# The last output projection of a two-block transformer: twelve of its sixteen column tiles in pairs, by seven products of halves

## What is computed

```python
def odd_layer(x, norm_g, w_in, q_gain, k_gain, sinks, w_out, rel_bias):
    h = rms_norm_2(x, norm_g) @ w_in
    q, k, v, gate = split_cols_2(h, ODD_SPLITS)
    ...
    o = swa_sink_attention(q, k, v, sinks, rel_bias)
    return x + (jax.nn.silu(gate) * o) @ w_out        # [512,2048] @ [2048,2048]
```

## Time and profile before

| | us |
|---|---|
| median of 3 runs (lowest, highest) | 2705.16 (2702.83, 2705.91) |
| the profiled execution | 2701.84 |
| its span | 2700.1 |
| PE busy | 2657.8 (98%) |
| DVE, ACT, POOL busy | 1139.1 (42%), 993.2 (37%), 1262.3 (47%) |

### The profile page before, as it was taken

The page is one execution under the profiler, slowest core; times in us unless marked ns, Lnnn a source line. Parts: engine busy times, 40 slices in busy tenths (PEclk is TensorE's granted clock), DMA queues, the critical chain, the costliest instruction groups (busy, mean ns, idle before and its releaser), DMA issues.

```text
span 2700.1 us, 34253 instructions
## 1 busy us (share of the span) xinstructions
PE 2657.8 (98%) x13651; PEld 2136.9 (79%) x13651; DVE 1139.1 (42%) x1857; ACT 993.2 (37%) x1582; POOL 1262.3 (47%) x655
## 2 busy tenths in 40 slices
PE   7999999999999999999999999999999999999999
PEld 4678988888888777888877778677888887777887
DVE  3257344146530427322123577554223445666311
ACT  4342522242242335322233123664222335666311
POOL 1236135235513537455433445776564555444443
PEclk9999999999999999999999999999999999999999
DMA  9853253225682322365332333324443333222543
GB/s 369 312 187 107 79 159 82 60 83 194 190 120 67 94 63 78 92 147 133 98 95 78 103 85 100 89 78 138 125 123 96 92 92 100 79 79 79 152 118 89
DMA packets 502237, 317.38 MB, mean 118 GB/s; under 512 B 100560, under 2 KB 456656, under 8 KB 499264
## 3 DMA queue, kind: packets, MB, share of 16 engines
q1 hardware_dynamic: 444720, 280.66, 36.2%
q10 hardware_dynamic: 57360, 34.54, 5.5%
HBM read 298.26 MB, written 29.41 MB: 121 GB/s over the span
## 4 chain that ended last, share of the span: by engine, by line
PE 94%; POOL 2%; DVE 1%; ACT 1%; issue 1%; SPq 1%; DMA 1%; DVEq 0%; ACTq 0%; POOLq 0%
PE acc L2252 81%; PE aux L2252 7%; PE ssq L2255 3%; PE ssq L2252 2%; POOL w_lo L1364 1%; DMA ada_ring<-in_w_ada 1%; DVE rstd L1719 0%; PE aux L2255 0%; SPq L773 0%; ACT p_t L1181 0%; ACT w_hi L1033 0%; POOL nbr_bias L1434 0%; POOL staged_lo L1381 0%; DVE gate_rows L1812 0%; PE acc L2255 0%
## 5 line engine op out<-in xcount | busy, mean ns | idle before, releaser
L1364 POOL TENSOR_TENSOR w_lo<-raw,w_hi 128x1024 fp32r<-128x1024 f32 x362 | 877.7, 2425 | 1221.4 <-ACT w_hi L1033 1221.3
L2252 PE MATMUL acc<-h_hi,w_hi 128*128 128x512 f32 (+1 forms) x3232 | 1188.1, 384 | 4.5 <-DVE k_t L1731 1.5
L2252 PE MATMUL acc<-h_hi,w_lo 128*128 128x512 f32 (+1 forms) x3232 | 1170.6, 379 | 0.0
L2252 PE MATMUL acc<-h_lo,w_hi 128*128 128x512 f32 (+1 forms) x2464 | 872.0, 376 | 0.0
L1033 ACT ACTIVATE w_hi<-raw 128x1024 fp32r<-128x1024 f32 x362 | 383.8, 1060 | 1057.6 <-PE acc L2252 1034.1
L2252 PEld LDWEIGHTS acc<-h_hi,w_hi 128*128 128x128 f32 x3232 | 583.9, 188 | 152.0 <-issue 34.9
L2252 PEld LDWEIGHTS acc<-h_hi,w_lo 128*128 128x128 f32 x3232 | 583.7, 188 | 117.3
L2252 PEld LDWEIGHTS acc<-h_lo,w_hi 128*128 128x128 f32 x2464 | 439.9, 188 | 82.5 <-issue 1.9
L2252 PE MATMUL acc<-out_t_lo,w_hi 128*128 128x512 f32 x768 | 298.8, 389 | 0.0
L1719 DVE RECIPROCAL rstd<-rstd 128x512 f32<-128x512 f32 (+1 forms) x29 | 118.0, 4070 | 271.3 <-ACT rstd L1085 271.2
L2252 PEld LDWEIGHTS acc<-out_t_lo,w_hi 128*128 128x128 f32 x768 | 144.2, 188 | 29.5
(11 more groups left out here) (300 smaller groups left out, 2614.5 us busy)
## 6 DMA issues: line engine op xcount, KB each, us to landing
raw<-in_w_in SPq DMA_DIRECT2D x52, 1024.0 KB, 5.9
raw<-in_even_w_in SPq DMA_DIRECT2D x41, 1024.0 KB, 5.6
raw<-in_odd_w_in SPq DMA_DIRECT2D x36, 1024.0 KB, 5.6
ada_ring<-in_w_ada SPq DMA_DIRECT2D x32, 1024.0 KB, 6.0
gate_ring<-in_w_ada SPq DMA_DIRECT2D x16, 1024.0 KB, 6.4
raw<-in_w_out SPq DMA_DIRECT2D x16, 1024.0 KB, 6.4
raw<-in_even_w_out SPq DMA_DIRECT2D x16, 1024.0 KB, 5.9
raw<-in_odd_w_out SPq DMA_DIRECT2D x16, 1024.0 KB, 5.8
```

Source lines behind the costliest of these rows:

```text
L1364: G_.tensor_tensor(WL[half][:], RAW[G.rs][:, half * HALF * P:(half + 1) * HALF * P], WH[half][:].bitcast(F32), ALU.subtract).then_inc(S["l ...
L2252: return M.matmul(out_, lhsT, rhs, start=start, stop=stop, skip_group_check=True)
```

## The change

Tiles 0 to 3 of the last stage stay as they were ("whole tiles"). Tiles 4 to 15 are done as six pairs. A pair's weights are four blocks of 1024 x 128 (a, c the upper half of the rows for the two tiles, b, d the lower half), and the gated input is four quarters (two halves of the rows, two of the tokens). A pair is then a product of 2 x 2 blocks by 2 x 2 quarters, and is done by seven products in place of eight, in the scheme of Strassen and Winograd, with s1 = c + d, s2 = s1 - a, s3 = a - c, s4 = b - s2 on the weights' side and four sums t1 to t4 on the input's. A product is 8 k-tiles x 3 matmuls of 256 columns, with its own rounded and split factor.

- The sums of the input, once: DVE makes them in two sets of eight operations (`hidden_sums`), ahead of the additions of whole tiles 1 and 2; t2, t3 and t4 are left in PSUM (`acc`, `aux`, `ssq`) and t1 in SBUF, in the place of the last four tiles of `x_t`. ACT rounds them (`sums_hi`, ahead of the stores of tiles 1 and 2), DVE makes their low parts (`hidden_lo`). t1 takes the place of the quarter it isn't needed with, so its two parts are made after the whole tiles.
- The sums of the weights, for each pair: four operations of DVE, s1 in `aux`, s2 in `ssq`, s3 and s4 in place.
- The factors: ACT rounds seven for a pair; POOL splits a, b, s3, s4 and d, DVE s2 and s1. There is a third pair of buffers for them.
- DVE adds each product's result to `x_t` (seven additions of 256 columns for a pair), then transposes the two tiles.
- SP loads blocks of 0.5 MB into a ring of six; the last load of `x_t` stands between block c and block d of pair 1 and waits until t1 is used up.

```diff
-    for j in range(KT):
+    for j in range(WHOLE):
...
+WHOLE = 4
+PAIRS = (KT - WHOLE) // 2
+PRODUCTS = ("a", "b", "s2", "s1", "s3", "s4", "d")
+BY_POOL = (0, 1, 4, 5, 6)
+BLOCK_AT = {"a": 0, "c": 1, "d": 2, "b": 3}
...
+        def wblock(s, what):
+            at_ = (4 * s + BLOCK_AT[what]) % 6
+            ring = (RAWX, RAW[third.rs], RAW[fourth.rs])[at_ // 2]
+            return ring[:, at_ % 2 * HALF * P:(at_ % 2 + 1) * HALF * P]
+        def factor(s, n):
+            return {"a": wblock(s, "a"), "b": wblock(s, "b"), "s2": SSQ[:], "s1": AUX[:], "s3": wblock(s, "c"),
+                    "s4": wblock(s, "b"), "d": wblock(s, "d")}[PRODUCTS[n]]
+        def halves(s, n):
+            slot = (7 * s + n) % 3
+            return (WHX, WLX) if slot == 2 else (WH[slot], WL[slot])
...
+        def sums_of(s, n):
+            at_ = {0: 0, 1: 768, 2: 0, 3: 512, 4: 0, 5: 512, 6: 0}[n]
+            return ACC[:, (third.c + s) % 2, at_:at_ + 256]
...
+            def pairs():
+                for s in range(PAIRS):
+                    if s == 0:
+                        sp.wait_ge(S["half_done"], gates_done)
+                    elif s == 1:
+                        sp.wait_ge(S["lo_done"], 2 * fourth.g + 2)
+                    else:
+                        sp.wait_ge(S["lo_done"], lo_pool(s - 2, 6))
+                    load(s, "a")
+                    load(s, "c")
+                    if s == 1:
+                        sp.wait_ge(S["h_full"], KT + 7)
+                        x_four(2, 3)
+                    if s == 0:
+                        sp.wait_ge(S["lo_done"], 2 * third.g + 2)
+                    else:
+                        sp.wait_ge(S["w_sums"], 4 * s - 1)
+                        sp.wait_ge(S["lo_done"], lo_pool(s - 1, 0))
+                    load(s, "d")
+                    if s:
+                        sp.wait_ge(S["lo_done"], lo_pool(s - 1, 4))
+                    load(s, "b")
...
-                        for b in range(4):
-                            sp.dma_start(tiles(X, KT, SEQ)[:, 4 * b:4 * b + 4],
-                                         xt_d[G.layer - 1][4 * b:4 * b + 4].rearrange("k p t -> p k t"))\
-                              .then_inc(S[f"xl{b}"], 16)
+                        for b in range(4 if G.kind == "wout" else 3):
+                            x_four(G.layer, b)
...
+                def sums_hi(half):
+                    act.wait_ge(S["w_fin"], 32)
+                    act.wait_ge(S["h_sum"], KT + 8 * half + 8)
+                    for t in ("t2", "t3", "t4"):
+                        (by_bank if t == "t2" else whole_bank)(lambda o, i: A.activation(o, i, ACT.Copy),
+                                                               four_k(three(SUMH[t][:]), half), SUMP[t])                            .then_inc(S["hf_hi"], 1)
+                def factor_hi(s, n):
+                    what = PRODUCTS[n]
+                    if what in "abd":
+                        act.wait_ge(block_sem(what), loaded_block(s))
+                    else:
+                        act.wait_ge(S["w_sums"], 4 * s + {"s2": 2, "s1": 2, "s3": 3, "s4": 4}[what])
+                    if 7 * s + n < 2:
+                        act.wait_ge(S["half_done"], 2 * fourth.g + n + 1)
+                    elif 7 * s + n > 2:
+                        act.wait_ge(S["half_done"], number(s, n - 3))
+                    A.activation(halves(s, n)[0][:], factor(s, n), ACT.Copy).then_inc(S["hi_done"], 1)
+                def pairs():
+                    for s in range(PAIRS):
+                        for n in range(7):
+                            factor_hi(s, n)
+                            if s == 0 and n == 2:
+                                act.wait_ge(S["half_done"], products_before)
+                                A.activation(quarter(H3H, 0, 1), three(SUM1[:]), ACT.Copy).then_inc(S["hf_hi"], 1)
+                            if s and n in (3, 4):
+                                send(WHOLE + 2 * s - 5 + n)
+                        if s == 0:
+                            send(WHOLE - 1)
+                    for j in (KT - 2, KT - 1):
+                        send(j)
...
+                    if G is third or G is fourth:
+                        sums_hi(int(G is fourth))
...
+                for s in range(PAIRS):
+                    for n in BY_POOL:
+                        high, low = halves(s, n)
+                        pool.wait_ge(S["hi_done"], number(s, n))
+                        G_.tensor_tensor(low[:], factor(s, n), high[:].bitcast(F32), ALU.subtract)\
+                          .then_inc(S["lo_done"], 1)
...
-                        need(dve, "fin_turned", j - 1)
-                        Vv.tensor_tensor(FIN[G.js][:], a, ktile(X, j, SEQ), ALU.add).then_inc(S["taken"], 1)
-                        need(dve, f"out{G.js}", 64 * (j // 2))
-                        dve.wait_ge(S["taken"], G.t + 1)
-                        Vv.transpose(FOUT[G.js][:], FIN[G.js][:]).then_inc(S["fin_turned"], 1)
+                        Vv.tensor_tensor(ktile(X, j, SEQ), a, ktile(X, j, SEQ), ALU.add).then_inc(S["taken"], 1)
+                        block_turn(j, G.t + 1)
...
+                def hidden_sums(half):
...
+                    def made_of(to, one, two, op, after_):
+                        dve.wait_ge(S["h_sum"], count + after_)
+                        split = by_bank if any(t is SUMP["t2"] for t in (to, one, two)) else whole_bank
+                        split(lambda o, a, b: Vv.tensor_tensor(o, a, b, op), to, one, two).then_inc(S["h_sum"], 1)
+                    if half == 0:
+                        dve.wait_ge(S["half_done"], gates_done)
+                        dve.wait_ge(S["ot_lo"], 2 * KT)
+                        dve.wait_ge(S["w_pt0"], 32)
+                    else:
+                        dve.wait_ge(S["h_full"], KT + 3)
+                    whole = lambda to, n, after_: made_of(to, lows[n].bitcast(F32), highs[n].bitcast(F32), ALU.add, after_)
+                    whole(rest, 1, 0)
+                    whole(t3, 0, 0)
+                    made_of(t1, rest, t3, ALU.subtract, 2)
+                    whole(t2, 3, 0)
+                    made_of(t3, t2, rest, ALU.subtract, 4)
+                    made_of(t2, t2, t1, ALU.subtract, 5)
+                    whole(rest, 2, 5)
+                    made_of(t4, rest, t2, ALU.subtract, 7)
...
+                def hidden_lo(t, half, rounded_):
+                    dve.wait_ge(S["hf_hi"], KT + rounded_)
+                    (by_bank if t == "t2" else whole_bank)(
+                        lambda o, a, b: Vv.tensor_tensor(o, a, b, ALU.subtract), four_k(three(SUML[t][:]), half), SUMP[t],
+                        four_k(three(SUMH[t][:]), half).bitcast(F32)).then_inc(S["h_full"], 1)
...
+                def hidden_steps(j):
+                    if j == 1:
+                        hidden_sums(0)
+                    elif j == 2:
+                        for n, t in enumerate(("t2", "t3", "t4")):
+                            hidden_lo(t, 0, n + 1)
+                        hidden_sums(1)
+                    elif j == 3:
+                        hidden_lo("t2", 1, 4)
+                        hidden_lo("t3", 1, 5)
+                        hidden_lo("t4", 1, 6)
+                        dve.wait_ge(S["h_full"], KT + 6)
+                        weight_sums(0)
+                        weight_difference(0)
...
+                def weight_sums(s):
+                    for what in "acd":
+                        dve.wait_ge(block_sem(what), loaded_block(s))
+                    need(dve, "xg_lo", lo_dve(s - 1, 3) if s else 0)
+                    weight_sum(AUX[:], wblock(s, "c"), wblock(s, "d"), ALU.add, 4 * s)
+                    weight_sum(SSQ[:], AUX[:], wblock(s, "a"), ALU.subtract, 4 * s + 1)
+                def weight_difference(s):
+                    weight_sum(wblock(s, "c"), wblock(s, "a"), wblock(s, "c"), ALU.subtract, 4 * s + 2)
...
+                def factor_lo(s, n):
+                    high, low = halves(s, n)
+                    dve.wait_ge(S["hi_done"], number(s, n))
+                    Vv.tensor_tensor(low[:], factor(s, n), high[:].bitcast(F32), ALU.subtract).then_inc(S["xg_lo"], 1)
...
+                def add_product(s, n, tile, half, after_):
+                    at_ = (WHOLE + 2 * s + tile) * SEQ + 256 * half
+                    dve.wait_ge(S["half_done"], number(s, n))
+                    need(dve, "taken", taken_before + 7 * s + after_ if after_ else 0)
+                    Vv.tensor_tensor(X[:, at_:at_ + 256], sums_of(s, n), X[:, at_:at_ + 256], ALU.add)\
+                      .then_inc(S["taken"], 1)
...
+                def pairs():
+                    for s in range(PAIRS):
+                        dve.wait_ge(S[f"xl{(WHOLE + 2 * s) // 4}"], 256 + 32)
+                        factor_lo(s, 2)
+                        add_product(s, 0, 0, 0, 0)
+                        if s == 0:
+                            dve.wait_ge(S["hf_hi"], KT + 7)
```

(74 more changed lines are left out.)

58 lines of the change are left out of this document (45 added, 13 removed).

## The result

The changed kernel takes 2715.6 us (median of 5; 2713.81 to 2720.02), the kernel before beside it 2702.83: a ratio of 1.0051, 95% interval 1.0037 to 1.0066. It is 12.8 us slower; 2713 was forecast, 8.2 slower than the 2705.16 that the forecast started from. The profiled execution had 2713.81, against 2701.84 before.

What follows compares the result with a forecast made beforehand. TensorE was taken to bound the kernel (94% of the span). Terms −9.5 − 0.3 + 5.3 + 4.7 + 0.5 + 4.1 + 3.4 = +8.2 us on the median of 2705.16 gave 2713; range 2703 to 2720.

Steps and rivals of the forecast that it cites:

- Matmuls, gain 9.5: Tiles 4 to 15: 1008 matmuls of 256 columns at 0.12 us, 121.0 instead of 130.5 us, gain 9.5.
- The rival of 0.11: The 42 products: narrow matmuls stream at 0.11 us, worth 10.1 us, giving −1.9 and 2703; chance 13%.
- Sums in PSUM that don't wait, a rival: VectorE's input sums: those written into PSUM don't wait for GpSimd; 4.0 us less, +4.2, 2709; chance 20%.
- First pause, 5.3: Ahead of tile 3: waits for GpSimd delay VectorE's sums, so it starts at 27.1 instead of 21.8.
- Start of the pairs, 42.7: Product 0 starts 42.7 us after tile 0's matmuls instead of 32.6, its factor rounded behind tile 2's stores.
- second pause: Ahead of product 0: PE waits 4.7 us from tile 3's end at 38.0 for the first factor.
- The 0.5 behind it: Behind the pairs' start: VectorE's difference of weights, 42.6 to 43.8, holds the next split; 0.5 us.
- Product 4 at 58.9: First pair: late block d and VectorE's sums delay product 4 from 54.8 to 58.9, a pause of 4.1 us.
- the other case: Ahead of product 4: GpSimd's split, asking at 56.1, goes before VectorE's sums; third pause 6.6 instead of 4.1 us.
- Clock, 3.4, bounds 0 and 6.8: TensorE at half clock after the second and third pauses, 1.7 us lost each, 3.4 in all.
- Steady pairs: Pairs after the way in: no pauses, 20.2 us each, costed at nothing; the rival that they don't hold had 10%.
- third pause: Ahead of product 4 of the first pair: x_t's load holds up block d; 4.1 us, 6.6 if GpSimd goes first.

Runs made afterwards that it cites:

- e3: Changed kernel with x_t's last load behind blocks d and b, and a PSUM operand replacing the low quarter in eight input sums; 0.9986 of the kernel before.
- e4: Changed kernel with x_t's last load behind d and b, six whole tiles, five pairs, sums rounded between weight halves; 1.0026 of the kernel before.
- e7: Changed kernel with 48 unused matmuls of 256 columns on PE in each of the second and third pauses; 1.0032 of the kernel before.
- e5: e4 with a whole tile's stores behind the next tile's weights in ScalarE's queue and tile 2 ahead of the second sums; 0.9972 of the kernel before.
- e8: e5 with the pairs' first factor in the free third buffer and pair 1's weight sums behind an addition of pair 0; 0.9967 of the kernel before.

## Why the prediction was right, step by step

- **Matmuls, gain 9.5:** 1008 × 0.1200 = 121.0, so 9.6 by the trace. The rival of 0.11 falls. The Trainium skill (TensorE: Matmul & The Clock Gate, Back-to-back issue gap) has 109 ns for 256 columns, but as the gap of a matmul by itself, which the prediction set beside a stream; the stream here has 120.0.
- **Sums in PSUM that don't wait, a rival:** falls; sums into `aux` lasted 3.2 to 3.4 beside a split. The sentence of the Trainium skill (SBUF — State Buffer, Who interferes with whom) that puts the condition on the inputs agrees with this, and with e3's 1.22.
- **First pause, 5.3:** mis-sized, 2.3. Tile 1's addition came as forecast (17.0), though the terms given for it add up to 17.7 (1.6 + 10.2 + 0.4 + 2.1 + 2.1 + 1.3). But I let the stores hold ScalarE for 2.0 behind the roundings of the sums. In the timeline the stores' issues (`ACTq`) run beside these roundings, and the next rounding comes only 0.44 late:

```profile
2549.53 1.05 ACT L1409 ACTIVATE h_sum_hi_t<-ssq 128x1024 fp32r<-128x1024 f32 x1
2549.83 1.09 ACTq L684 DMA_DIRECT2D out<-final_nat  x2
2551.02 1.06 ACT L1145 ACTIVATE w_hi<-raw 128x1024 fp32r<-128x1024 f32 x1 [0.44 <-issue]
```

In e4, where no rounding ran beside the four stores, the next one came 2.1 behind the first of them. And since ScalarE was earlier, GpSimd's split asked ahead of VectorE's next two sums (2552.16 against 2552.37) and not behind them.

- **Start of the pairs, 42.7:** 43.0, partly by luck. VectorE's second set ended at 36.0 instead of 33.8, because it waited for GpSimd twice, 2.0 and 2.2, and not once for 1.0. But the roundings of the sums took 2.9 instead of 3.3, and tile 2's stores held ScalarE for 0.45 and not for 2.0, so the first factor's rounding started only 0.4 late:

```profile
2566.58 1.09 ACT L1409 ACTIVATE h_sum_hi_t<-acc 128x512 fp32r<-128x512 f32 x2 [13.03 <-DVE ssq L2298]
2569.95 1.06 ACT L1423 ACTIVATE w_hi<-raw_more 128x1024 fp32r<-128x1024 f32 x1 [0.45 <-issue]
```

Tile 3 ended earlier than in my walk, so the second pause was 6.1 instead of 4.7; the start was set by VectorE and not by tile 3. The 0.5 behind it didn't come ahead of product 1, whose split was ready before product 0, at half clock, ended; 0.4 came ahead of product 3, for a low part that VectorE makes.

- **Product 4 at 58.9:** the term that was too small; it started at 64.5, 5.6 later. x_t's load was issued 3.4 later than in my walk, mostly since VectorE waited for GpSimd in two sums of pair 0's weights (3.22 and 2.01 instead of 1.2), where I had counted no wait. Block d landed 7.4 behind that issue, not 6.9. And GpSimd's split came first, which I had as the other case: 2.95 instead of 1.2. That is 3.4 + 0.5 + 1.75.
- **Clock, 3.4, bounds 0 and 6.8:** half clock for 10.2 us from t = 38.9 and 6.8 from 62.8, longer than I took, but with 2.3 of price by e7. I had added it to the second pause without asking what is late next.
- **Steady pairs:** nothing, as forecast.
- **Sum:** by parts −9.6 + 10.4 (start of the pairs) + 3.5 (products 0 to 3, 15.0 instead of 11.5) + 6.5 (third pause) + 2.3 (the other 38, 111.8 instead of 109.4, the clock's price) = 13.1 in the trace, and 0.3 back at the end. The medians give 12.8, the forecast was 8.2. The mechanisms were the forecast ones and the sign rests on them. The size was short by 4.6, most of it at product 4 (64.5, where the sum had 58.9 and 1.7 of clock): the third pause came later and longer, with GpSimd's split first, which I had kept for the upper bound only. The 2713 lies nearer to 2715.6 than the 8.2 does to the 12.8, because the kernel before had 2702.83 beside the changed one, and not the 2705.16 that the forecast started from.

## What to carry to other kernels

Work taken from the engine that bounds is worth what the engine that gets it can do in the time: here the waits between VectorE and GpSimd put off the pairs by nine to ten us, about as much as the matmuls gained. A step moved into an in-order queue brings its waits with it; look at every instruction behind it, stores included, before moving it. And a way in wants cover: two more tiles done the old way cost 1.6 us. Cover alone was not enough: in e4's order the stage grew by 3.6, and only with the stores behind the weights did the long pauses go (e5), and in e8 all of them.
